# One layer of a hybrid encoder: four up tiles along the x1 chain, second norm's sums a tile later

## What is computed

```python
def block_tail(x, mix, g_mix_post, g_ffn_pre, g_ffn_post, w_up, w_down):
    x = x + rms_norm(mix, g_mix_post)
    h = rms_norm(x, g_ffn_pre)
    f = jnp.square(jax.nn.relu(h @ w_up)) @ w_down
    return x + rms_norm(f, g_ffn_post)
```

## Time and profile before

| | |
|---|---|
| median of three runs | 893.11 us |
| profiled execution, its own time | 894.82 us |
| its span | 893.0 us |
| PE busy | 865.8 us (97% of the span) |
| DVE, ScalarE, GpSimd busy | 474.3, 303.6, 69.0 us |
| mean granted clock of TensorE | 0.988 |

### The profile page before, as it was taken

The page is one execution under the profiler, slowest core; times in us unless marked ns, Lnnn a source line. Parts: engine busy times, 40 slices in busy tenths (PEclk is TensorE's granted clock), DMA queues, the critical chain, the costliest instruction groups (busy, mean ns, idle before and its releaser), DMA issues.

```text
span 893.0 us, 16412 instructions
## 1 busy us (share of the span) xinstructions
PE 865.8 (97%) x6866; PEld 850.1 (95%) x6866; DVE 474.3 (53%) x729; ACT 303.6 (34%) x448; POOL 69.0 (8%) x53
## 2 busy tenths in 40 slices
PE   6999999999999999999996899999999999999997
PEld 6999999999989999999995899999999999999997
DVE  6325779776735546656426654774433443334434
ACT  5211645354531112335323342123311332123432
POOL 1000101100020000000224400000000000000122
PEclk9999999999999999999996999999999999999999
DMA  9322212221313131123231022232222222322212
GB/s 311 105 95 94 86 59 72 88 90 59 96 48 101 54 101 49 54 95 95 95 94 49 18 79 95 95 94 95 82 64 89 94 94 94 94 91 66 80 48 101
DMA packets 77405, 77.28 MB, mean 87 GB/s; under 512 B 2912, under 2 KB 75120, under 8 KB 77360
## 3 DMA queue, kind: packets, MB, share of 16 engines
q1 hardware_dynamic: 68416, 70.53, 24.5%
q10 hardware_dynamic: 8304, 3.95, 1.6%
q0 software_dynamic: 640, 2.17, 0.7%
HBM read 71.64 MB, written 4.99 MB: 86 GB/s over the span
## 4 chain that ended last, share of the span: by engine, by line
PE 92%; DVE 5%; issue 1%; DMA 1%; ACT 1%; SPq 0%; DVEq 0%; ACTq 0%
PE acc L715 76%; PE wk L715 3%; PE wk L739 3%; PE wk L844 3%; DVE act_lo L1372 1%; DMA x_nat<-in_x_prompt 1%; PE wk L805 1%; PE wk L806 1%; PE wk L914 1%; DVE scaled L1353 1%; PE wk L922 1%; DVE w_lo L1065 1%; PE wk L912 0%; PE acc L1043 0%; PE acc L1045 0%
## 5 line engine op out<-in xcount | busy, mean ns | idle before, releaser
L452 ACT ACTIVATE w_hi<-w_raw 128x1024 fp32r<-128x1024 f32 x123 | 130.4, 1060 | 473.8 <-PE acc L715 455.5
L715 PE MATMUL acc<-act_hi,w_hi 128*128 128x272 f32 x1200 | 254.6, 294 | 10.8 <-DVE act_lo L1372 8.6
L715 PE MATMUL acc<-act_hi,w_lo 128*128 128x272 f32 x1200 | 249.8, 290 | 0.0
L715 PE MATMUL acc<-act_lo,w_hi 128*128 128x272 f32 x1200 | 249.1, 289 | 0.0
L715 PEld LDWEIGHTS acc<-act_hi,w_hi 128*128 128x128 f32 x1200 | 190.2, 190 | 16.0 <-DVE act_lo L1372 10.0
L715 PEld LDWEIGHTS acc<-act_lo,w_hi 128*128 128x128 f32 x1200 | 190.3, 190 | 0.0
L715 PEld LDWEIGHTS acc<-act_hi,w_lo 128*128 128x128 f32 x1200 | 188.9, 190 | 0.0
L1065 DVE TENSOR_TENSOR w_lo<-w_raw,w_hi 128x1024 fp32r<-128x1024 f32 x123 | 151.7, 1233 | 35.5 <-ACT w_hi L452 35.0
L715 PE MATMUL acc<-mid_hi,w_hi 128*128 128x272 f32 x480 | 99.0, 287 | 0.0
L715 PE MATMUL acc<-mid_hi,w_lo 128*128 128x272 f32 x480 | 98.7, 288 | 0.0
L715 PE MATMUL acc<-mid_lo,w_hi 128*128 128x272 f32 x480 | 98.6, 287 | 0.0
(11 more groups left out here) (219 smaller groups left out, 985.4 us busy)
## 6 DMA issues: line engine op xcount, KB each, us to landing
w_raw<-in_w_in SPq DMA_DIRECT2D x44, 512.0 KB, 4.4
w_raw<-in_w_ff_up SPq DMA_DIRECT2D x32, 512.0 KB, 4.7
w_raw<-in_w_ff_down SPq DMA_DIRECT2D x32, 512.0 KB, 4.0
w_raw<-in_w_o SPq DMA_DIRECT2D x8, 512.0 KB, 4.5
x_nat<-in_x_prompt SPq DMA_DIRECT2D x4, 512.0 KB, 5.7
w_raw<-in_w_attn_out SPq DMA_DIRECT2D x4, 512.0 KB, 3.6
w_raw<-in_w_ret_out SPq DMA_DIRECT2D x4, 512.0 KB, 4.5
out_y_prompt<-x_nat SPq DMA_DIRECT2D x3, 512.0 KB, 3.1
```

Source lines behind the costliest of these rows:

```text
L452: act.activation(w_hi[:, v % 2], w_raw[:, v // 2, :, P * (v % 2):P * (v % 2) + P], ACT.Copy).then_inc(hi_ready, 1)
L715: ins = pe.matmul(dst[:, n, 0:HALF], w[:, k, :], h[:, HALF * n:HALF * n + HALF], start=begin, stop=end)
```

## The change

- **First group.** All four up tiles of group 15 are made along the x1 chain, each in its own PSUM tile: for every k PE does the 16 matmuls that need only the high part, then the 8 with the low part. Their four weight blocks (`first_hi`, `first_lo`) are split by ScalarE and DVE in the sixth and seventh w_o tile. When a tile is done, ScalarE copies it to SBUF (`early`), and group 16 follows on PE.
- **First norm.** `sum_over` sums with a 128 by 128 matrix of ones, in f32, so that every partition holds every token's sum; ScalarE takes the root of 128 by 544, DVE the reciprocal of 128 by 544 (`rstd_over`). The epsilon is put into `sqsum` beforehand. The last w_o tile is squared from PSUM.
- **x1 chain.** DVE does all eight adds. ScalarE writes the squares of x1 to `y_mix`; GpSimd adds them after the last low part.
- **Second norm.** PE's sums stand in the second tile of group 16, ahead of its third step; root and reciprocal as in the first norm.
- **First hidden tiles.** DVE reads them from `early` when the second norm's `rstd` is there. No weight split stands between them; the first two blocks of group 16 are split ahead by name, the next by `up` of group 16.

```diff
+        first_at = [z_at + 4 * T * s for s in (Z_RK, Z_RV, Z_RG)]
+        first_hi = [place(f"first_hi{q}", [P, KT, P], fr, at=first_at[q])[:] for q in range(3)] + [w_hi_third[:]]
+        first_lo = [place(f"first_lo{q}", [P, KT, P], fr, at=first_at[q] + 8 * T)[:] for q in range(3)] + [w_lo_third[:]]
...
+        early = [part_a[:], part_b[:], merged[:, 0, :], merged[:, 1, :]]
+        std = relu2[:, 0, :]
...
-            order.after(pool.memset(sqsum[:], 0.0))
+            order.after(pool.memset(sqsum[:], EPS * D / P))
             for m in range(KT - 1):
                 add_square(1, m)
 
             pool.wait_ge(sum_mm, 1)
-            order.after(pool.memset(sqsum[:], 0.0))
-            for m in range(KT):
-                if m % 2:
-                    pool.wait_ge(scaled_ready, m // 2 + 1)
-                    pool.tensor_tensor(xT[:, m, :], xT[:, m, :], scaled[:, m % 4, :], ALU.add).then_inc(x1_odd, 1)
-                if m > 1:
-                    add_square(2, m - 2)
-            add_square(2, KT - 2)
+            order.after(pool.memset(sqsum[:], EPS * D / P))
+
+            pool.wait_ge(h2_lo, KT)
+            for m in range(KT - 1):
+                pool.tensor_tensor(sqsum[:], sqsum[:], y_mix[:, m, :], ALU.add).then_inc(sq_added, 1)
+                pool.wait_ge(sq_added, squares_added(2, m + 1))
...
-            with act.Fori(0, 2) as i:
-                for j in range(4):
-                    split_ahead(i + G_WO, j)
-                    evacuated(act, i + G_WO, j)
-                    act.wait_ge(sq_added, 4 * i + j + 1)
-                    act.activation(sq[:, j % 2, :], y_mix[:, 4 * i + j, :], ACT.Square).then_inc(sq_ready, 1)
-
-            act.wait_ge(w_in_sem[1], 32 * (G_FFN + 1))
-            act.activation(w_hi_third[:], w_raw[:, 1, :, 0:P], ACT.Copy).then_inc(hi_ready, 1)
-            root(1)
+            def first_split(q):
+
+                act.wait_ge(w_in_sem[q // 2], 32 * (G_FFN + 1))
+                act.activation(first_hi[q], w_raw[:, q // 2, :, P * (q % 2):P * (q % 2) + P], ACT.Copy).then_inc(hi_ready, 1)
+
             for m in range(KT):
-                act.wait_ge((x1_even, x1_odd)[m % 2], m // 2 + 1)
+                g, j = G_WO + m // 4, m % 4
+                if m < KT - 2:
+                    split_ahead(g, j)
+                if m == KT - 3:
+                    first_split(0)
+                    first_split(1)
+                if m < KT - 1:
+                    evacuated(act, g, j)
+                    y = y_mix[:, m, :]
+                else:
+
+                    act.wait_ge(mm_done, 4 * g + j + 1)
+                    y = acc[1][:, :, 0:HALF]
+                act.wait_ge(sq_added, m + 1)
+                to = sq[:, m % 2, :]
+                act.activation(to if m < KT - 1 else halves(to), y, ACT.Square).then_inc(sq_ready, 1)
+                if m == KT - 2:
+                    first_split(2)
+                    first_split(3)
+
+            def std_over(norm):
+
+                act.wait_ge(sum_mm, norm)
+                act.activation(halves(std), wk_halves[0][:, :, 0:HALF], ACT.Sqrt, scale=1.0 / D).then_inc(std_ready, 1)
+
+            std_over(1)
+            for m in range(KT):
+                act.wait_ge(x1_ready, m + 1)
                 act.activation(act_hi[:, m, :], xT[:, m, :], ACT.Copy, scale=gains[:, 2, m:m + 1]).then_inc(h2_hi, 1)
-                if m >= 2:
-
-                    act.wait_ge(sq_added, squares_added(2, m - 1))
-                act.activation(sq[:, m % 2, :], xT[:, m, :], ACT.Square).then_inc(sq_ready, 1)
-            root(2)
+                act.activation(y_mix[:, m, :], xT[:, m, :], ACT.Square).then_inc(sq_ready, 1)
+                if m == KT - 4:
+                    split_hi(4 * G_FFN + 4, 0, 32 * (G_FFN + 2))
+            dst = [wk_halves[0], acc[0], acc[1], wk_halves[1]]
+            for q in range(4):
+                act.wait_ge(mm_done, 4 * G_FFN + q + 1)
+                act.activation(halves(early[q]), dst[q][:, :, 0:HALF], ACT.Copy).then_inc(early_read, 1)
+            split_hi(4 * G_FFN + 5, 1)
+            std_over(2)
...
             def up(c, i, first=False):
                 for j in range(4):
                     g = G_FFN + 4 * c + i
-                    if not (first and j < 2):
+                    if not first:
                         split_ahead(g, j)
                     k = 8 * c + 4 * i + j
...
-            split_ahead(G_FFN, 1)
             up(0, 0, first=True)
             up(0, 1)
...
+            def sum_over(norm):
+
+                last = sq[:, 1, :] if norm == 1 else y_mix[:, KT - 1, :]
+                for src, count, value in ((sqsum[:], sq_added, squares_added(norm, KT - 1)), (last, sq_ready, KT * norm)):
+                    pe.wait_ge(count, value)
+                    for n in range(2):
+                        ins = pe.matmul(wk_halves[0][:, n, 0:HALF], ones[:], src[:, HALF * n:HALF * n + HALF],
+                                        start=count is sq_added, stop=count is sq_ready)
+                ins.then_inc(sum_mm, 1)
...
-            feature_sum(1, squares_added(1, KT - 1), KT)
...
-            for k in range(KT):
+            sum_over(1)
+
+            pe.wait_ge(lo_ready, 4 * G_FFN + 4)
+            pe.wait_ge(acc_free, 4 * G_FFN + 2)
+            pe.wait_ge(std_ready, 2)
+            dst = [wk_halves[0], acc[0], acc[1], wk_halves[1]]
...
+            def first_product(q, k, w, h, start=False, stop=False):
+
+                for n in range(2):
+                    ins = pe.matmul(dst[q][:, n, 0:HALF], w[:, k, :], h[:, HALF * n:HALF * n + HALF], start=start, stop=stop)
+                return ins
+
+            for k in range(KT - 1):
+                pe.wait_ge(h2_hi, k + 1)
+                for q in range(4):
+                    first_product(q, k, first_hi[q], H_HI[k], start=k == 0)
+                    first_product(q, k, first_lo[q], H_HI[k])
                 pe.wait_ge(h2_lo, k + 1)
-                for j in range(2):
-                    if k == 0:
-                        pe.wait_ge(lo_ready, 4 * G_FFN + j + 1)
-                        pe.wait_ge(acc_free, 4 * G_FFN + j + 1)
-                    ins = products(acc[j], w_hi[:, j], w_lo[:, j], k, H_HI[k], H_LO[k], k == 0, k == KT - 1)
-                    if k == KT - 1:
-                        ins.then_inc(mm_done, 1)
-            feature_sum(2, squares_added(2, KT - 1), 2 * KT)
-            pe.wait_ge(lo_ready, 4 * G_FFN + 3)
-            for k in range(KT):
-                if k == 3:
-                    spread(2)
-                ins = products(wk_halves[1], w_hi_third, w_lo_third, k, H_HI[k], H_LO[k], k == 0, k == KT - 1)
-            ins.then_inc(mm_done, 1)
-
-            pe.wait_ge(acc_free, 4 * G_FFN + 4)
-            column_tile(G_FFN, 3, H_HI, H_LO)
+                for q in range(4):
+                    first_product(q, k, first_hi[q], H_LO[k])
+            pe.wait_ge(h2_lo, KT)
+            for q in range(4):
+                first_product(q, KT - 1, first_hi[q], H_HI[KT - 1])
+                first_product(q, KT - 1, first_lo[q], H_HI[KT - 1])
+                first_product(q, KT - 1, first_hi[q], H_LO[KT - 1], stop=True).then_inc(mm_done, 1)
+
+            def second_norm(k):
+
+                if k == KT // 4:
+                    pe.wait_ge(early_read, 1)
+                    sum_over(2)
+
+            for j in range(4):
+                if j < 2:
+                    pe.wait_ge(early_read, 2 + j)
+                column_tile(G_FFN + 1, j, H_HI, H_LO, before=second_norm if j == 1 else None)
...
-            up(G_FFN + 1)
             down(0)
...
-                if between:
-                    between()
-                dve.wait_ge(*((spread_mm, n + 1) if n <= 2 else (tok_rstd_ready, n + 1)))
-                if keep:
-                    order.after(dve.tensor_copy(rstd[:], wk[:, 0:T]))
+                dve.wait_ge(tok_rstd_ready, n - 1)
+
+            def rstd_over(n):
+
+                dve.wait_ge(std_ready, n + 1)
+                order.after(dve.reciprocal(rstd[:], std))
...
-            def third_low():
...
-            with dve.Fori(0, 2) as i:
-                for j in range(4):
-                    dve.wait_ge(mm_done, 4 * (i + G_WO) + j + 1)
-                    copy(y_mix[:, bass.ds(4 * i + j, 1), :].rearrange("p a (n c) -> p (a n) c", n=2), acc[j % 2][:, :, 0:HALF])\
-                        .then_inc(acc_free, 1)
-                    split_ahead(i + G_WO, j)
-            norm(1, between=third_low)
...
-            def pair(p, between=None):
...
-                if p:
-                    scale(p, 1).then_inc(scaled_ready, 1)
-                if between:
-                    between()
-                order.after(scale(p, 0))
-                dve.tensor_tensor(xT[:, 2 * p, :], xT[:, 2 * p, :], scaled[:, 2 * (p % 2), :], ALU.add).then_inc(x1_even, 1)
-                if p == 0:
-                    scale(p, 1).then_inc(scaled_ready, 1)
...
+            def first_low(q):
+
```

(60 more changed lines are left out.)

34 lines of the change are left out of this document (11 added, 23 removed).

## The result

The changed kernel takes 898.23 us (median of eight runs, 896.64 to 898.88). In the same eight rounds the kernel before takes 893.78. The ratio is 1.0047, with a 95% interval of 1.0035 to 1.0059: slower by 4.45 us, which is more than a measurement of this kernel is uncertain. The profiled execution took 896.71 us, with a span of 894.9 us.

The account below looks back on a forecast made before the run. PE's work bounds the kernel except in one low-clock slice, where the chain after the last w_o tile does. Terms summed to 76.97 us against 71.58, 5.4 more on the median 893.11: 898.5 us, range 890.5 to 902.1.

Parts of the forecast that it names:

- (a): First norm's sums on PE: two pairs of f32 matmuls at 1.0 us a pair, 2.0 us.
- (b): First norm's square root over 544 columns on ScalarE: 0.66 us and a hand-over, 0.7 us.
- (g): Second norm: sums 2.0 us, root 0.7, reciprocal 4.7, while PE runs the rest of the second tile.
- (c): First norm's reciprocal over 544 columns on DVE: 4.65 us at 8.3 ns a column, 4.7 with hand-overs.
- (d): Scale, add and act_hi of x1's tile 0, before PE's first up product: 2.34 us.
- (e): First group's four up tiles on PE: 24.05 us plus 1.6 lost to a low-clock start, 25.65 us.
- (f): PE goes straight on with the second up group, 7.51 us until the sums; GpSimd's adds end 4 us earlier.
- (h): Third tile's weight split queued behind four serial hidden tiles of 2.77 us each, 11.1 us.
- (i): DVE's relu and weight split after the hidden tiles, 1.95 us; PE waits 14 us before the third tile.
- (j): Second up group's third and fourth tiles: 12.02 us plus 1.6 from the low clock, 13.62 us.
- rival 2: Clock stays low longer: both restarts cost 3.0 us, sums 1.2 a pair; 9.0 us slower, 902.1; chance 0.10.
- likeliest case: The forecast itself, 898.5 us, with chance 0.65; its own range 896.3 to 902.1 us.

Follow-up runs that it names:

- recip_plain: The changed kernel with both 128x544 reciprocals replaced by plain multiplications of the same size; 892.03 us, ratio 0.9985 to the kernel before.
- all_warm: all_three plus 44 matmuls nobody reads in PE's pause before the first up product; 882.55 us, ratio 0.9879 to the kernel before.
- sums_early: The changed kernel with the second norm's sums six steps of k earlier, in the group's first tile; 892.70 us, ratio 0.9991 to the kernel before.
- relu_ahead: The changed kernel with DVE's relu of hidden tile j+1 ahead of the low part of tile j; 893.71 us, ratio 0.9993 to the kernel before.
- weights_ahead: The changed kernel with the third and fourth tiles' weight splits ahead of the hidden tiles, and own PSUM tiles for these two; 892.90 us.
- all_three: The changed kernel with sums_early, relu_ahead, and weights_ahead's PSUM tiles and its splits at other places; 882.94 us, ratio 0.9884 to the kernel before.
- gp_beside: The changed kernel with GpSimd adding each x1 square when ready, beside DVE's chain; 899.63 us, ratio 1.0073 to the kernel before.
- pe_warm: The changed kernel with 90 matmuls nobody reads in PE's wait before the second up group's third tile; 895.44 us, ratio 1.0021.

## Why the prediction was right, step by step

The forecast was 898.5 us and the range 890.5 to 902.1. Sign, mechanism and sum hold, and two terms of the sum, the reciprocal and the second restart, were mis-sized in opposite directions. That the time came within 0.3 us is luck in part: the stretch grew by 4.4 us and not by 5.4, and the kernel before, from whose 893.11 the forecast starts, measured 893.78 in the rounds of the result.

- **(a), (b), (g) sums and roots.** 1.91 and 1.85 against 2.0, 0.63 against 0.66: the middle value between the two bounds was right.
- **(c), (g) the reciprocal.** The term that was most off: 3.55 us against 4.65, so 1.1 less, twice. Two points of 2 and 5 columns gave 8.3 ns a column where 6.1 to 6.5 are right: a slope from 25 ns of difference over three columns, drawn out over 539. The choice of the dearer end was right in direction, and recip_plain shows that the sign hung on it. The Trainium skill, "VectorE: DVE Perf Modes", section "First, the fixed hardware budget", gives a repeat count of 8, from which the prediction estimated 4.7 us or 0.7 by two readings. The rows agree with neither; they lie nearer to the first.
- **(d), (e) the first tile and the four tiles.** 2.47 against 2.34, and 26.07 against 25.65. PE runs from 480.08 to 506.15 without another wait, after a cold start of some 3.5 us (480.08 to about 483.6), and DVE's tile at 2.31 us stays under PE's 3.0. The half that gains is there: 34.7 us to the end of the four tiles, where it was 47.5.
- **(f)** 7.52 against 7.51, and GpSimd's adds end 5.8 us early. all_warm shows how thin such a cover is: with the sums 4.5 us earlier and PE faster it was gone.
- **(h), (i) the second stall.** The wait was 12.8 against 14; with a reciprocal of 3.55 the sum of (i) gives 12.9. Its parts are as told: four rounds of 2.77, then 1.90 against 1.95. recip_plain, sums_early, relu_ahead and weights_ahead each take away one of the things that it consists of, and all_three the whole.
- **(j)** 14.81 against 13.62. The clock stayed low for 5.5 us instead of 3.6, a loss of 2.5 for the 1.6 taken. This is a part of rival 2, in one of the two restarts.

The two reciprocals give −2.2, (e) and (j) +0.4 and +1.2, and the rest is −0.2 in sum: 76.97 becomes 76.15. To put the difference on the median and not on the profiled execution was right: the two profiled executions differ by 2.2 us ahead of the change. The lower end of the likeliest case, 896.3, is added up wrongly: four pairs of sums at 0.5 less are 2.0 and not 1.8, half a cold loss of 1.6 is 0.8 and not 0.4, so it is 895.7; the range, which reaches down to 890.5, doesn't rest on it.

The price set on GpSimd's silence came from an act_lo that took twice its time in the order of before. gp_beside shows that it is the add that pays in the new order, 1.16 us a tile, most of which PE's own pace hides. Not tried was the old order of the x1 chain with four tiles, so what the four tiles gain without the silence is known only from gp_beside: with GpSimd beside it the four tiles end 37.0 us after w_o (472.71 to 509.71), against 34.7 in the change and 47.5 before.

## What to carry to other kernels

When a stage is shortened by doing a later stage's work early, ask what the displaced result (here the second norm) feeds, and follow every engine's program from there to the next thing PE needs: the stall stood two tiles behind the change, in the order of DVE's and ScalarE's programs. Here waits of PE of 3.9 to 12.8 us cost their length and then a stretch at half clock, while behind waits of 1.4 and 1.5 us (all_warm, pe_warm) the clock stayed at 1.00. Reorderings that shorten the same wait added up: three of 4.5 to 5.5 us brought 15.3 together. A price that decides the sign and rests on a slope over a few columns should be measured by itself first.

## What the runs showed of the hardware that was not expected

- The reciprocal of f32 on DVE costs 6.1 to 6.5 ns a column between 136 and 544 columns (965, 1796 to 1854 and 3553 ns), against 0.72 us for an add of the same 544.
- DVE and GpSimd can hold each other up in either direction, by which of them starts first: GpSimd's add first, and DVE's takes 1.88 us for 0.72 (gp_beside); DVE's split first, and GpSimd's add takes 2.20 for 1.37 (all_warm).
- How long the clock stays low after a wait didn't follow the length of the wait in these profiles: 2.9 us after 8.3 (sums_early), 6.2 after 8.5 (relu_ahead), 5.5 after 12.8 (the change). By the spacing of pairs, 0.45 for 0.25, the first two differ by 1.5 us after waits of nearly the same length. Each is one execution, and executions of one kernel differ as much: the twelve of relu_ahead go from 891.61 us at a mean granted clock of 0.991 to 897.14 at 0.984, the profiled one. So the difference can't be put down to the two kernels.
- At the start of an execution the clock can be granted at once or later: 1.00 in the change's profile and 0.66 before, both from 15 to 20 us. Of the 2.2 us by which the two are apart from there on, 0.7 stand before the first product and 1.5 come up while the clock is low.
